# Order of two groups of fetches on GpSimd's queue, and of a latent's sums on TensorE

## The chip, the cores and the metric

The kernel runs on one core of a Trainium2 chip. The metric is the device time of one execution in microseconds (us), and the median over several runs counts.

## The reference

Two transformer blocks run one after the other on a sequence of 1024 positions with 1024 features, all in float32. The change lies in the first block, which reads in short:

```python
x = layer_norm(x, ln_emb_g, ln_emb_b)
z = x @ w_in
xs, gs, cq, ckv, kr, gm = split(z)             # 512, 512, 256, 128, 64, 512 columns
# state-space branch: 32 groups of 16 features with 64 complex states each
y = gelu(scan(xs) + d_skip * xs)
ys = y * sigmoid(y @ w_glu + b_glu) * silu(gs)
# latent attention, 4 heads: 128 plain and 64 rotary columns for queries and keys
q  = rms_norm(cq, q_norm_g) @ w_uq             # rotary(q[..., 128:])
kv = rms_norm(ckv, kv_norm_g) @ w_ukv
k_rope = rotary(kr)                            # one rotary key for all heads
ym = softmax(mask(q @ k.T) * scale) @ v * silu(gm)
u = alpha * x + concat(ys, ym) @ w_out
```

The second block (two more attentions, gates and a gated feed-forward part) follows from it.

## The kernel before, in words

Everything is kept with features on the 128 partitions and positions along the columns. On-chip memory is divided into 50 pages of 1024 float32 columns; a page has several uses one after the other. Each engine runs one instruction list written out by hand, and semaphores tie the lists together. The DMAs that matter here are issued from three lists: SyncE loads weight blocks into a ring of four pages, ACT stores the gates, and GpSimd issues the rest through its software queue.

The stage around the change, in TensorE's order:

- The last two of 16 column tiles of `w_in` (`in_tile(14)`, `in_tile(15)`). ACT takes each from its bank: tile 12 is the key/value latent `CKV`, tiles 13 and 14 are the two pages of the query latent `CQ`, tile 15 is the rotary rows `KR` (and the same rows with their halves exchanged).
- Sums of squares of the latents for their RMS norms. `latent_square_act` (L1003) squares a latent on ACT into `TEMPS_2[i]`, `latent_sums_pe` (L981) sums it with eight small products, `latent_root_act` takes the root, VectorE the reciprocal, and `latent_spread_pe` (L989) spreads it. Latent 0 is the key/value latent, 1 and 2 are the query's. For latents 1 and 2 the squares were both put in page 32, so the second square waits for the first one's sums.
- The state products, four groups `r` (L3282 and L3288), once VectorE says that the states are ready (`states_ready`, L2548). ACT copies each group's result to `UU` (L1929).
- Values and keys from the key/value latent (L3311, and four tiles by the helper at L3125), the four plain query tiles, and the two pairs of rotary query tiles, also at L3125. Of every key and query tile ACT makes a rounded high part, and VectorE the remainder (L2566 for keys, L2584 for queries). The second rotary pair waits for the remainders of all four plain query tiles (`q_low`, 4).
- The gated unit of the state-space branch, four tiles at L3125. It waits for `yg_ready`, the four Gelu activations of ACT (L1952) over `YF` (pages 12 to 15).
- The attention, whose scores begin at L355. It waits for VectorE's `rotary_ready`.

`YF` is the state-space output with features on partitions. `UU` has steps on partitions, so it goes to DRAM and comes back in another layout. GpSimd issues these: the store of `UU` to `y_dram` (L1650), and eight fetches of 256 KB each (L1660) for a quarter of a page's rows at a time. Between store and fetches stand four copies of the rotary rows `KR` (256 KB each, L1654 and L1655) into both halves of pages 46 and 47, and the fetch of the causal mask (L1656). Page 47 holds the half-angle sine until VectorE has made the cosine, so these copies wait for `cm_zero` (L1652), which VectorE reports after the rotary tables are finished (L2571). After the eight fetches have landed GpSimd fetches the gates (L1666, L1667).

VectorE, in its list, waits for the rotary rows (`kr_landed`) after the remainders of the first two plain query tiles. It then makes the rotary key (three operations at L2350, one at L2581, one more at L2350), and only then the last two query remainders:

```python
            for m in range(4):
                if m == 2:
                    dve.wait_ge(S("kr_landed"), 64)
                    dve.wait_ge(S("ssm_ps"), 32)
                    tt(page(46), page(46), COS, ALU.mult)
                    tt(page(47), page(47), SIN, ALU.mult)
                    tt(page(46), page(46), page(47), ALU.add)
                    link(dve.tensor_copy(KRH, page(46)))
                    tt(KRL, page(46), KRH.bitcast(F32), ALU.subtract)
                dve.wait_ge(*T("q_free", m + 1))
                dve.tensor_tensor(QNL[m], two(2 * (m % 2)), QNH[m].bitcast(F32), ALU.subtract).then_inc(S("q_low"), 1)
```

Of the kernel before, what the change touches and what calls it, by code (L numbers as in the profile page):

```python
# [19 lines left out]
PAGE = 1024  # L20
# [7 lines left out]
GROUPS, GC, STATE = 32, 16, 64  # L28
PAIRS = GROUPS // 2
STEP = P // GC  # L30
# [34 lines left out]
def program(nc, t, out):  # L65
    with ExitStack() as ctx:
        sems = {}

        def S(name):
            name = ONE_COUNT.get(name, (name, 0))[0]  # L70
            if name not in sems:
                sems[name] = ctx.enter_context(nc.semaphore(name))
            return sems[name]
# [9 lines left out]
        def cols(a, b, parts=P):  # L83

            if b <= FRONT * PAGE:
                return front[0:parts, a:b]
            return back[0:parts, a - FRONT * PAGE:b - FRONT * PAGE]
# [12 lines left out]
        def page(a, n=1, off=0):  # L100
            return cols(a * PAGE + off, (a + n) * PAGE + off)

        def pages(a, n):
            return page(a, n).rearrange("p (k t) -> p k t", k=n)
# [34 lines left out]
        YF = pages(12, 4)  # L139
# [38 lines left out]
        y_dram = nc.dram_tensor("ssm_out_by_step", (P, GROUPS, CHUNKS), F32, kind="Internal").ap()  # L178
# [203 lines left out]
        def attention_dve(dve, A, bufs, items, per_turn, turns, scale, before):  # L382
            SBUF, PTB = bufs
            n, step, used = len(items), 0, 0
            for what in steps_of(items, per_turn, turns):
# [3 lines left out]
                if isinstance(what, str):  # L389
                    _, dst, times = turns[int(what)]  # L390
                    dve.wait_ge(S(f"{A}_scores"), used)
                    if times is None:
                        dve.tensor_copy(dst, pair).then_inc(S(f"{A}_scores_read"), 1)
                    else:
                        dve.tensor_tensor(dst, pair, times, ALU.mult).then_inc(S(f"{A}_scores_read"), 1)
                    continue
# [354 lines left out]
        def tiles_to(N, k):  # L751
            names = list(NORMS)
            return sum(NORMS[x] for x in names[:names.index(N)]) + k
# [223 lines left out]
        def latent(i):  # L977

            return (CKV, "kv_norm", V("kv_norm_g", 0)) if i == 0 else (CQ[:, i - 1, :], "q_norm", V("q_norm_g", i - 1))

        def latent_sums_pe(pe, i):  # L981
            pe.wait_ge(S("norm_square"), tiles_to("kv_norm", i + 1))
            ones_, at = ones_q if i else ones_kv, 256 if i else 0
            for j in range(4):
                mm = pe.matmul(ps[32 * j:32 * j + 32, 7, at:at + 256], ones_[:, 0:32],
                               TEMPS_2[i][:, 256 * j:256 * j + 256], start=i < 2, stop=i != 1)
            mm.then_inc(S("norm_square_used"), 1)

        def latent_spread_pe(pe, N):  # L989
            pe.wait_ge(S("norm_rstd"), norms_to(N))  # L990
            if N == "q_norm":
                pe.wait_ge(S("norm_scaled"), tiles_to("kv_norm", 1))
            else:
                pe.wait_ge(S("ssm_ps_read"), 24)
            for j in (0, 2, 1, 3):
                at = slice(32 * j, 32 * j + 32)
                if j == 1:
                    mm.then_inc(S("half_spread"), 1)
                    pe.wait_ge(S("half_spread"), 2 if N == "q_norm" else 1)
                mm = pe.matmul(LATENT[:, j, :], pick[at, :], LATENT_ROOT[N][at, :], start=True, stop=True)  # L1000
            mm.then_inc(S("norm_spread"), 1)

        def latent_square_act(act, i):  # L1003
            if i:
                act.wait_ge(S("norm_square_used"), tiles_to("kv_norm", i))
            act.activation(TEMPS_2[i], latent(i)[0], ACT.Square).then_inc(S("norm_square"), 1)

        def latent_root_act(act, N, i):
# [4 lines left out]
        def latent_gain_act(act, i):  # L1013
            x, _, gain = latent(i)
            act.wait_ge(S("norm_scaled"), tiles_to("kv_norm", i + 1))
            act.activation(x, x, ACT.Copy, scale=gain).then_inc(S("norm_ready"), 1)
# [162 lines left out]
                x = quarters(XN[:, k, :])  # L1179
                dve.scalar_tensor_tensor(x, x, V("ln_emb_g", k), SPREAD, ALU.mult, ALU.mult).then_inc(S("norm_scaled"), 1)  # L1180

        TEMPS_2 = (cols(48 * PAGE + 512, 49 * PAGE + 512), page(32), page(32))
        LATENT_ROOT = {"kv_norm": cols(49 * PAGE + 512, 49 * PAGE + 768), "q_norm": cols(33 * PAGE, 33 * PAGE + 256)}
        STATE_BANK = (0, 1, 2, 3)
        K_BANK = (5, 0, 2, 5)
# [115 lines left out]
        def nth(b):  # L1301

            return whole(b) + len(GATES.order) * (b >= B_MERGE + 2 * N_GATES) + len(OUT.order) * (b >= B_UP) + \
                len(UP.order) * (b >= B_DOWN)
# [278 lines left out]
        def _(pool):  # L1583
# [64 lines left out]
            ada_sum(15)  # L1648
            pool.wait_ge(S("ssm_ps_read"), 32)
            pool.dma_start(y_dram, UU).then_inc(S("y_in_dram"), 16)  # L1650
            pool.wait_ge(S("z_free"), N_IN)
            pool.wait_ge(S("dve_step"), DVE_STEP["cm_zero"])  # L1652
            for half in range(2):
                pool.dma_start(page(46)[64 * half:64 * half + 64, :], KR[0:64, :]).then_inc(S("kr_landed"), 16)  # L1654
                pool.dma_start(page(47)[64 * half:64 * half + 64, :], KR[64:128, :]).then_inc(S("kr_landed"), 16)  # L1655
            pool.dma_start(CM[:, SEQ - P:SEQ], t["causal"]).then_inc(S("cm_landed"), 16)  # L1656

            pool.wait_ge(S("y_in_dram"), 16)
            for g in range(8):
                pool.dma_start(YF[g * GC:(g + 1) * GC, :, :].rearrange("c k (s n) -> c k s n", s=STEP),  # L1660
                               y_dram.rearrange("(s c) (k g) n -> g c k s n", c=GC, g=8)[g]).then_inc(S("yf_landed"), 16)
            pool.wait_ge(S("yf_landed"), 16 * 8)
            pool.wait_ge(S("gate_out0"), 64)
            pool.wait_ge(S("gate_out1"), 64)
# [147 lines left out]
        def _(act):  # L1812
# [98 lines left out]
            act.wait_ge(S("dve_step"), DVE_STEP["g_skip"])  # L1911
            act.wait_ge(S("z_free"), 13)
            latent_square_act(act, 0)
            in_high(act, 15)
            z(13, CQ[:, 0, :], ACT.Copy)
            latent_root_act(act, "kv_norm", 0)
            z(14, CQ[:, 1, :], ACT.Copy)
            act.wait_ge(S("z_free"), 15)
            act.wait_ge(S("dve_step"), DVE_STEP["states_ready"])
            latent_square_act(act, 1)  # L1920
            z(15, KR, ACT.Copy)
            latent_square_act(act, 2)
            latent_root_act(act, "q_norm", 2)
            latent_gain_act(act, 0)
# [1184 lines left out]
        def _(pe):  # L3109
# [22 lines left out]
            def ada_column(a, back):  # L3132

                pe.wait_ge(S("ada_summed"), a + 1)
                a0, n = [x for x in ADA_STAGES if x[0] <= a][-1]
                if a == a0 and a > 0:
                    pe.wait_ge(S("ada_read"), ADA_STAGES.index((a0, n)))
                pe.matmul(ps[:, 4, a - a0:a - a0 + 1], ring[:, ADA_BLOCKS[a] % RING, 0:P], ones[:, 0:1],
                          start=True, stop=True).then_inc(S(back), 1)
# [99 lines left out]
            for x in range(16, 24):  # L3239
                pe.wait_ge(S("ssm_ps_read"), x - 9)  # L3240
                q4, i = (x - 16) // 2, x % 2
# [22 lines left out]
            in_tile(14)  # L3264
            in_tile(15)
            pe.sem_inc(S("w_used"), B_UKV)
            latent_sums_pe(pe, 1)
            pe.wait_ge(S("dve_step"), DVE_STEP["states_ready"])
            pe.wait_ge(S("tm_landed"), 16 * (STEP - 1))
            for r in range(4):  # L3270
                if r < 2:
                    pe.wait_ge(S("z_free"), 15 + r)
                else:
                    pe.wait_ge(S("ssm_ps_read"), 22 + 2 * r)

                def state(j, odd):
                    return ps[:, STATE_BANK[2 * (r % 2) + odd], j * P:(j + 1) * P]

                for j in range(4):
                    for odd in range(2):  # L3280
                        g = 8 * r + 2 * j + odd
                        mm = pe.matmul(state(j, odd), TM[:, g, :], UU[:, g, :], start=j == 0, stop=False,  # L3282
                                       skip_group_check=True)
                for j in range(4):
                    for i in range(2):
                        for odd in range(2):
                            h, q = slice(64 * odd, 64 * odd + 64), 4 * r + j
                            mm = pe.matmul(state(j, odd), CP[h, i, q, GC:GC + P], SS[h, i, q, :], start=False,  # L3288
                                           stop=j == 3 and i == 1, skip_group_check=True)
                            if j == 3 and i == 1:  # L3290
                                mm.then_inc(S("ssm_ps"), 1)
                if r == 0:
                    latent_sums_pe(pe, 2)
                    latent_spread_pe(pe, "kv_norm")
                    ada_column(12, "ada_used")
                    ada_column(13, "ada_used")
                elif r == 1:
                    latent_spread_pe(pe, "q_norm")
                    ada_column(14, "ada_used")
                elif r == 2:  # L3300
                    ada_column(15, "ada_used")
# [266 lines left out]
            for i in range(4):  # L3568
                n = nth(B_MERGE + i)
# [13 lines left out]
            for m in range(8):  # L3583
                n, bank = nth(B_MERGE + 2 * N_GATES + m), 4 * (m % 2)
# [80 lines left out]
            for half in range(2):  # L3665
                n = nth(B_UP + 2 + half)
# [158 lines left out]
```

## Time and profile before

| | us |
|---|---|
| median of 3 runs | 2158.92 |
| lowest and highest run | 2156.01, 2160.89 |
| the profiled execution | 2164.66 |
| its span | 2162.8 |
| TensorE busy in the span | 2079.2 |
| VectorE, ACT, GpSimd busy | 1357.9, 818.0, 1141.4 |

The profile is of one execution, and its times count from the span's start. PE is TensorE, DVE is VectorE, POOL is GpSimd, SPq and the like are an engine's instruction queue. An idle time in square brackets stands before the instruction of its row, with what ended it. "x32" is the number of instructions merged in a row.

### The profile page before, as it was taken

The numbers are of one execution on the slowest core, as the hardware profiler recorded it, in microseconds if no ns is written. First come the engines' busy times: TensorE is split into PE (matmuls) and PEld (weight loads), VectorE is DVE, ScalarE is ACT, GpSimd is POOL, SyncE is SP. The second block draws the span as 40 slices with busy tenths as digits, with TensorE's granted clock in tenths as the row PEclk, the third lists the DMA queues.
The fourth block names the chain that finished last, engine by engine and source line by source line (L and its number), as shares of the span: only waits on it lengthen the run. The fifth ranks groups of instructions, "written<-read, shape, count | busy, mean of one in ns | idle before, by whom it ended". The sixth has DMA issues, their size and how long they took to land.

```text
span 2162.8 us, 28447 instructions
## 1 busy us (share of the span) xinstructions
PE 2079.2 (96%) x11124; PEld 1632.0 (75%) x11124; DVE 1357.9 (63%) x1705; ACT 818.0 (38%) x1304; POOL 1141.4 (53%) x793
## 2 busy tenths in 40 slices
PE   8999989999998999999999999998999999999997
PEld 5878745878875885578857788876788888887885
DVE  7999865541768015520067424775977777778988
ACT  6232242340117005620065343134544545453443
POOL 2576713057873663346646764374677778750000
PEclk9999999999998999999999999999999999999999
DMA  7463472042232321001211325333122222137543
GB/s 298 149 142 108 115 158 77 1 185 98 88 102 81 119 78 47 28 27 52 74 24 51 113 100 202 107 117 136 35 74 88 88 88 88 64 135 283 169 152 113
DMA packets 72726, 230.02 MB, mean 106 GB/s; under 512 B 15960, under 2 KB 18824, under 8 KB 71280
## 3 DMA queue, kind: packets, MB, share of 16 engines
q1 hardware_dynamic: 59632, 170.04, 23.8%
q10 hardware_dynamic: 9104, 36.45, 4.6%
q0 software_dynamic: 3856, 21.70, 4.0%
q8 instruction: 89, 1.46, 0.3%
q14 instruction: 45, 0.36, 0.1%
HBM read 180.03 MB, written 46.17 MB: 105 GB/s over the span
## 4 chain that ended last, share of the span: by engine, by line
PE 74%; DVE 16%; ACT 4%; issue 2%; POOL 2%; DMA 2%; SPq 0%; ACTq 0%; DVEq 0%; POOLq 0%
PE ps L3563 22%; PE ps L3160 17%; PE ps L3678 8%; DVE back L2350 6%; PE ps L3487 4%; PE ps L3596 4%; PE ps L3634 2%; PE ps L355 2%; PE ps L3125 2%; PE ps L525 1%; PE ps L513 1%; PE ps L378 1%; PE ps L1050 1%; DMA back<-ssm_out_by_step 1%; PE ps L507 1%
## 5 line engine op out<-in xcount | busy, mean ns | idle before, releaser
L1779 POOL TENSOR_TENSOR up_parts<-front,up_parts 128x512 fp32r<-128x512 f32 x120 | 188.5, 1580 | 74.8 <-ACT up_parts L2087 74.0
L3678 PE MATMUL ps<-ffn_parts,w_parts 128*128 128x512 f32 x924 | 212.6, 392 | 5.0 <-DVE ffn_parts L2946 5.0
L3678 PEld LDWEIGHTS ps<-ffn_parts,w_parts 128*128 128x128 f32 x924 | 174.2, 189 | 42.7 <-DVE w_parts L2938 3.8
L3563 PE MATMUL ps<-t_high,up_parts 128*128 128x512 f32 x640 | 204.0, 390 | 1.2 <-ACT back L2094 0.8
L3160 PE MATMUL ps<-h_high,w_parts 128*128 128x512 f32 x672 | 187.7, 394 | 0.6 <-PE ps L3487 0.6
L1704 POOL TENSOR_TENSOR w_parts<-front,sb_zero 128x1024 fp32r<-128x1024 f32 x48 | 101.9, 2123 | 158.4 <-PE ps L3487 58.1
L3563 PE MATMUL ps<-h_high,up_parts 128*128 128x512 f32 x480 | 154.8, 389 | 0.3 <-DVE back L2755 0.2
L1709 POOL TENSOR_TENSOR w_parts<-front,w_parts 128x1024 fp32r<-128x1024 f32 x54 | 141.9, 2628 | 19.9 <-ACT w_parts L2252 7.5
L3160 PEld LDWEIGHTS ps<-h_high,w_parts 128*128 128x128 f32 x672 | 124.0, 188 | 25.8 <-issue 1.4
L3563 PEld LDWEIGHTS ps<-t_high,up_parts 128*128 128x128 f32 x640 | 120.1, 188 | 27.1 <-issue 1.5
L1590 POOL TENSOR_TENSOR front<-front,sb_csilu 128x1024 f32<-128x1024 f32 x48 | 102.6, 2137 | 61.2 <-DMA front<-w_ada 61.1
L2350 DVE TENSOR_TENSOR back<-back 128x1024 f32<-128x1024 f32 (+10 forms) x72 | 104.9, 1457 | 36.9 <-ACT back L1984 19.5
L1594 POOL TENSOR_TENSOR front<-front 128x512 f32<-128x512 f32 x96 | 120.9, 1259 | 7.5
L3563 PE MATMUL ps<-t_low,up_parts 128*128 128x512 f32 x320 | 124.5, 389 | 0.0
L3563 PEld LDWEIGHTS ps<-h_high,up_parts 128*128 128x128 f32 x480 | 90.1, 188 | 19.7 <-issue 1.1
L3160 PE MATMUL ps<-h_low,w_parts 128*128 128x512 f32 x336 | 103.8, 390 | 0.0
L2755 DVE TENSOR_TENSOR back<-ps,back 128x512 f32<-128x512 f32 x78 | 53.1, 681 | 79.9 <-PE ps L3563 49.4
L2922 DVE SCALAR_TENSOR_TENSOR back<-back,sb_vec 128x1023 f32<-128x1023 f32 x40 | 60.8, 1519 | 52.0 <-ACT back L2232 52.0
L3563 PE MATMUL ps<-h_low,up_parts 128*128 128x512 f32 x240 | 93.4, 389 | 0.0
L2925 DVE SCALAR_TENSOR_TENSOR back<-back,sb_vec 128x1023 f32<-128x1023 f32 x40 | 86.6, 2166 | 1.4
L2094 ACT ACTIVATE back<-ps 128x512 f32<-128x512 f32 x98 | 57.9, 590 | 76.9 <-PE ps L3563 76.8
L614 POOL TENSOR_SCALAR back<-back,sb_na_inv 128x512 f32<-128x512 f32 x64 | 43.8, 698 | 81.6 <-DVE sb_na_inv L580 81.6
(445 smaller groups left out, 5039.6 us busy)
## 6 DMA issues: line engine op xcount, KB each, us to landing
front<-w_ada SPq DMA_DIRECT2D x48, 512.0 KB, 3.6
front<-w_up SPq DMA_DIRECT2D x44, 512.0 KB, 4.2
front<-w_down SPq DMA_DIRECT2D x22, 512.0 KB, 3.7
back<-w_down SPq DMA_DIRECT2D x22, 512.0 KB, 4.4
front<-w_in SPq DMA_DIRECT2D x16, 512.0 KB, 3.9
front<-w_out SPq DMA_DIRECT2D x16, 512.0 KB, 4.5
residual<-back ACTq DMA_DIRECT2D x2, 4096.0 KB, 14.9
front<-w_gates SPq DMA_DIRECT2D x16, 512.0 KB, 4.2
```

The source lines that it names most:

```text
L1590: pool.tensor_tensor(rows, rows, csilu[:].unsqueeze(2).to_broadcast((P, FT, P)), ALU.mult)\
L1594: pool.tensor_tensor(x[:, 0:w], x[:, 0:w], x[:, w:2 * w], ALU.add).then_inc(S("ada_step"), 1)
L1704: pool.tensor_tensor(high, raw, zero[:, 0:1].to_broadcast((P, PAGE)), ALU.add)\
L1709: pool.tensor_tensor(low, raw, high.bitcast(F32), ALU.subtract).then_inc(S("w_split"), 1)
L1779: pool.tensor_tensor(parts[:, BANK:], src, parts[:, 0:BANK].bitcast(F32), ALU.subtract)\
L2350: link(dve.tensor_tensor(o, a, b, op))
L2925: dve.scalar_tensor_tensor(y[:, :SEQ - 1], src[:, 1:], one(conv, n + ((4 + half) * N_UP)), y[:, :SEQ - 1], ALU.mult, ALU.add).then_inc(S(" ...
L3160: mm = pe.matmul(ps[:, bank + nt, :], w_[:, k * P:(k + 1) * P], x_[k][:, nt * BANK:(nt + 1) * BANK], start=k == 0 and n == 0, stop=k == FT ...
L3487: mm = pe.matmul(ps[:, 2 * j + nt, :], WR[n % 2 + w_][:, at:at + P], x_[2 * b + k][:, nt * BANK:(nt + 1) * BANK], start=b == 0 and k == 0 ...
L3563: mm = pe.matmul(o, parts[:, at + k * P:at + (k + 1) * P], x, start=p in (1, 2, 5) and k == 0 and q == 0, stop=k == 3 and q == 2, skip_gro ...
L3596: mm = pe.matmul(ps[:, bank + k // 4 * 2 + nt, :], WR[n % 2 + w_][:, k * P:(k + 1) * P], x_[k][:, nt * BANK:(nt + 1) * BANK], start=k % 4 ...
L3678: mm = pe.matmul(ps[:, (4 if p in (2, 5, 3) else 0) + m, :], weights[:, w_ * BANK + m * P:w_ * BANK + (m + 1) * P], half_of(x, x_), start= ...
```

## The change

Three things change. GpSimd issues the eight fetches of the states, with the wait for the store's landing, directly behind the store, and the rotary rows and the mask behind them. TensorE takes the sums of latent 1 behind the first group of state products and ahead of the sums of latent 2, instead of before that group. The square of latent 2 goes to page 34, and ACT's wait for the former latent's sums falls away.

```diff
         def latent_square_act(act, i):
-            if i:
-                act.wait_ge(S("norm_square_used"), tiles_to("kv_norm", i))
             act.activation(TEMPS_2[i], latent(i)[0], ACT.Square).then_inc(S("norm_square"), 1)
...
-        TEMPS_2 = (cols(48 * PAGE + 512, 49 * PAGE + 512), page(32), page(32))
+        TEMPS_2 = (cols(48 * PAGE + 512, 49 * PAGE + 512), page(32), page(34))
...
             pool.wait_ge(S("ssm_ps_read"), 32)
             pool.dma_start(y_dram, UU).then_inc(S("y_in_dram"), 16)
+            pool.wait_ge(S("y_in_dram"), 16)
+            for g in range(8):
+                pool.dma_start(YF[g * GC:(g + 1) * GC, :, :].rearrange("c k (s n) -> c k s n", s=STEP),
+                               y_dram.rearrange("(s c) (k g) n -> g c k s n", c=GC, g=8)[g]).then_inc(S("yf_landed"), 16)
             pool.wait_ge(S("z_free"), N_IN)
             pool.wait_ge(S("dve_step"), DVE_STEP["cm_zero"])
             for half in range(2):
                 pool.dma_start(page(46)[64 * half:64 * half + 64, :], KR[0:64, :]).then_inc(S("kr_landed"), 16)
                 pool.dma_start(page(47)[64 * half:64 * half + 64, :], KR[64:128, :]).then_inc(S("kr_landed"), 16)
             pool.dma_start(CM[:, SEQ - P:SEQ], t["causal"]).then_inc(S("cm_landed"), 16)
-
-            pool.wait_ge(S("y_in_dram"), 16)
-            for g in range(8):
-                pool.dma_start(YF[g * GC:(g + 1) * GC, :, :].rearrange("c k (s n) -> c k s n", s=STEP),
-                               y_dram.rearrange("(s c) (k g) n -> g c k s n", c=GC, g=8)[g]).then_inc(S("yf_landed"), 16)
             pool.wait_ge(S("yf_landed"), 16 * 8)
...
             pe.sem_inc(S("w_used"), B_UKV)
-            latent_sums_pe(pe, 1)
             pe.wait_ge(S("dve_step"), DVE_STEP["states_ready"])
...
                 if r == 0:
+                    latent_sums_pe(pe, 1)
                     latent_sums_pe(pe, 2)
                     latent_spread_pe(pe, "kv_norm")
                     ada_column(12, "ada_used")
```

## Rows read from the trace of the kernel before

**Rows 1.** The page: span, and the last chain's shares by engine.

```profile
span 2162.8 us, 28447 instructions
PE 74%; DVE 16%; ACT 4%; issue 2%; POOL 2%; DMA 2%; SPq 0%; ACTq 0%; DVEq 0%; POOLq 0%
```

**Rows 2.** The last chain in order of time, 225 to 345: start, us, what.

```profile
251.25 0.03 DVEq L2548
...
251.35 1.07 ACT back L1006
...
252.46 0.64 PE ps L985 x8
...
298.52 19.46 DMA back<-ssm_out_by_step
...
318.01 3.90 ACT back L1952 x4
```

**Rows 3.** Timeline of PE, 235 to 475: start, us, instruction, idle before.

```profile
257.00 0.64 PE L985 MATMUL ps<-back,sb_ones_q 128*32 128x256 f32 x8
...
303.34 13.97 PE L3125 MATMUL ps<-back,front 128*128 128x512 f32 x32 [0.40 <-PE ps L3125]
321.96 16.49 PE L3125 MATMUL ps<-back,front 128*128 128x512 f32 x32 [4.65 <-ACT back L1952]
...
352.87 0.36 PE L355 MATMUL ps<-k_high,q_high 128*128 128x256 f32 x1
```

**Rows 4.** Windows of PE: us, PE busy (count), PEclk, DMA share, GB/s.

```profile
320.00:321.00 1.00, 0.00 (x0) 0.59 0.78 164
...
326.00:327.00 1.00, 1.00 (x2) 0.50 0.96 360
327.00:328.00 1.00, 1.00 (x4) 1.00 1.01 414
...
473.00:474.00 1.00, 0.56 (x2) 0.89 1.15 492
...
477.00:478.00 1.00, 1.00 (x5) 0.90 0.80 344
```

**Rows 5.** Timeline of POOL, 245 to 325.

```profile
274.64 0.61 POOL L1650 DMA_DIRECT2D ssm_out_by_step<-back  x1 [8.77 <-ACT back L1929]
291.52 0.53 POOL L1654 DMA_DIRECT2D back<-back  x1 [16.27 <-DVEq L2572]
...
294.13 5.43 POOL L1660 DMA_DIRECT2D back<-ssm_out_by_step  x8
318.27 0.79 POOL L1666 DMA_DIRECT2D back<-first_gates  x1 [18.71 <-DMA back<-ssm_out_by_step]
```

**Rows 6.** DMA view, 274.6 to 281.3: issues, KB each, us to landing.

```profile
ssm_out_by_step<-back POOLq DMA_DIRECT2D x1, 2048.0 KB, 6.6
```

**Rows 7.** Timeline of ACT, 235 to 345.

```profile
253.22 1.05 ACT L1006 ACTIVATE back<-back 128x1024 f32<-128x1024 f32 x1
```

**Rows 8.** DMA view, 291.5 to 318.1: queue, packets, MB, share of 16 engines; issues.

```profile
q0 software_dynamic: 992, 3.21, 85.0%
q1 hardware_dynamic: 144, 0.52, 9.7%
...
front<-w_out SPq DMA_DIRECT2D x1, 512.0 KB, 15.2
```

**Rows 9.** DMA view, 303 to 313: the only data queue with a row.

```profile
q0 software_dynamic: 357, 1.16, 104.3%
```

**Rows 10.** Timeline of DVE, 297 to 345.

```profile
298.91 3.74 DVE L2350 TENSOR_TENSOR back<-back 128x1024 f32<-128x1024 f32 x3 [0.53 <-DMA back<-back]
...
304.68 2.35 DVE L2584 TENSOR_TENSOR q_low<-ps,q_high 128x1024 fp32r<-128x1024 f32 x2
310.48 2.48 DVE L2350 TENSOR_TENSOR back<-ps,back 128x1024 f32<-128x1024 f32 x2 [3.45 <-PE ps L3125]
```

**Rows 11.** The second and fourth row copy (L1655): issue to landing.

```profile
DMA to landing us min/median/max: 4.1/5.0/5.8
```

## The prediction

> **What bounds the kernel now.** The page's shares of the chain that ended last come first: 74% of it is TensorE's [rows 1]. So a change pays only where TensorE stands still, or stops standing still, on that chain. The chain, read in order of time around the changed lines, has one place that is not an engine at work. The last of the eight transfers that bring the states back from DRAM is out for 19.46 us, and the four Gelu activations follow it [rows 2]. TensorE's timeline shows what this costs: the second pair of query rotary products ends at 303.34 + 13.97 = 317.31 and the gated unit's products start at 321.96, a gap of 4.65 us [rows 3]. The granted clock then adds a second cost. It falls during that gap and is at half speed (1.2 instead of 2.4 GHz) until 327.0, so that 5.04 us of products at half speed do 2.52 us of work [rows 4]. Gap and clock together cost 7.2 us. The attention starts at 352.87 [rows 3], and everything later hangs on it.
>
> GpSimd's timeline says why the states come so late. Their store is issued at 274.64 [rows 5] and lands 6.6 us later, at 281.24 [rows 6]. The first fetch is issued only at 294.13, because the four rotary-row copies (from 291.52 on) and the mask stand ahead of it [rows 5], and these wait for the rotary tables.
>
> **The change, part by part.**
>
> *First latent sums behind state group 0.* VectorE reports the states ready at 251.25, but TensorE waits for the square, which ACT ends at 252.42 and whose sums take 0.64 us; the state products start at 253.10 [rows 2]. Afterwards they can start when ACT could, at 251.35: 1.75 us earlier. The eight sums then stand beside the third latent's. That group's row says 0.64 us [rows 3], and a little of it overlaps with its neighbours, so the net is between 1.1 and 1.2 us; I take 1.2. Nothing eats this up: squares and copies on ACT are done in time (the last square is at 253.22 + 1.05 = 254.27 [rows 7], the sums start at 255.3 at the earliest). So TensorE, ACT's copies, the store to DRAM and the rotary tables all come 1.2 us sooner.
>
> *Second square in a page of its own, its wait gone.* The square that waited starts at 253.22 [rows 7], 0.12 us after the sums on which it waited end (253.10 [rows 2]). The removed wait is worth between 0 and 0.1 us; I take 0. Its purpose is to allow the first edit: otherwise the square would wait for sums that have moved behind the state group.
>
> *Fetches ahead of the rotary rows.* The same 13 transfers are issued, in another order. The store now lands at 281.24 - 1.2 = 280.04. GpSimd resumes 0.28 us after a landing (317.99 to 318.27 [rows 2, 5]), so the first fetch goes out at 280.3 and the last by 285.8 (5.43 us for eight [rows 5]). The wait for the rotary tables ends as before, less 1.2, so the rotary rows are still issued from 291.52 - 1.2 = 290.3. They are issued no later, but behind 2 MB of states in the same queue (eight times 256 KB). No other work on GpSimd is queued behind this wait except the fetch of the gates, which waits for the states in both versions.
>
> How long does the queue take? From the first issue at 291.52 to the last landing at 317.98 are 26.46 us. In that stretch the software queue used 85.0% of 26.6 us of all 16 engines, and the hardware queue 9.7%, that is 2.6 us for 0.52 MB, one weight block [rows 8]. The same work started at 280.3 ends at 306.8. The mask (64 KB) is the last of it; as an estimate I take off 0.5 us for it and have the rotary rows landing at 306.3 if one weight block is served before them, at 303.7 if none is, and at 308.9 if two are. Two are asked for in that time (one of the gated unit, one of the output). For none speaks that the one output block asked for in that stretch took 15.2 us to land [rows 8], and that from 303 to 313 the software queue alone used 104.3% [rows 9], with no row for the hardware queue beside it. For one speaks that the block did move before the queue had drained. I take 305.0, in the middle. The states themselves need at most until 304 and their Gelu 3.9 us more [rows 2], so they no longer set anything.
>
> *What is late next.* VectorE waits for the rotary rows ahead of the last two query remainders, and the second rotary product pair on TensorE waits for those remainders, since it reuses their banks. Before, the rows were there at 298.9, the five rotary operations ran to 304.68 and the remainders to 307.03 [rows 10], ahead of TensorE, which reached the second pair at 303.34 + 6.98 = 310.32 [rows 3]. Now: rows at 305.0, five operations (5.77), two remainders (2.35), small steps between engines (0.1) give 313.2. TensorE gets there at 310.32 - 1.2 = 309.1. So a new gap of 4.1 us opens in place of the old one, one product pair earlier.
>
> *The sum.* Second pair 6.98 us. Clock loss 2.5 us again, as for a gap of like length [rows 4]. Step to the gated unit 0.35. From its start to the attention's it is 352.87 - 321.96 = 30.91 [rows 3], less the 2.52 that the clock took, so 28.4. Together 313.2 + 7.0 + 2.5 + 0.35 + 28.4 = 351.4, against 352.87. The gain is **1.4 us**. VectorE's two rotary passes over the queries have seven operations each, none above the 1.24 us of their first two [rows 10], so the second pass, which can start at 313.2 + 7.0 + 2.5 = 322.7, ends by 331.4, far ahead of 351. The gates, fetched behind the rotary rows, land before TensorE's first gated tile is through, so VectorE's multiplications wait for nothing new. From the attention on the shift is handed down by TensorE.
>
> In one formula: gain = 306.4 minus the landing of the rotary rows, plus 2.5 minus the clock loss. With 303.7 and 308.9 this gives a gain of 2.7 and a loss of 2.5. The clock loss is bounded from below by another gap: after 2.0 us of idleness the clock was at half from about 473.9 to 477.1, 3.2 us, a loss of 1.6 [rows 4]; from above I allow 3.3. Both ends together: 3.6 us faster to 3.3 us slower.
>
> The profiled execution took 2164.66 us with a span of 2162.8 [rows 1]; the sum gives 2163.3 for it. The median of the runs is 5.7 us below that execution, and the difference is carried over: 2158.9 - 1.4 = 2157.5 us. This kernel's runs lie within about 0.1% of their median, so some 0.2% (4.3 us) can be told from no change.
>
> **The rivals.**
>
> *A: the wait moves to the rotary rows (my forecast), 0.50.* 1.4 us faster, own range 3.6 faster to 2.5 slower: 2155.3 to 2161.4.
>
> *B: the rotary rows aren't held up, 0.12.* If they pass the states in the queue and land near 299 as before, TensorE has no gap: second pair 309.1 to 316.1, gated unit from 316.4 at full clock, end 344.8. That is 8.1 us faster, 2150.8. Against it: before, the transfers landed in the order of their issue. The four row copies were through by 298.9 (the fourth 5.8 us after issue), the last states at 318.0, 19.5 after theirs [rows 2, 11]. The Trainium skill (DMA: Bandwidth & Descriptors, section on queues, rings and completion order) says that each engine takes descriptors in ring order but that completion need not follow issue; the first half would hold the rows behind the states, the second would let them overtake by a few packets at most.
>
> *C: the weights are served first, 0.18.* The mechanism is the share of the hardware queue. If both blocks get their turn while the software queue is full, the rotary rows land at 308.9 and the kernel is 2.5 us slower, 3.3 with the longer clock loss: 2161.4 to 2162.2. It decides from a landing after 306.4, and passes 0.2% from 310.7 on. Against it stands the starved output block [rows 8, 9]. The Trainium skill (same page and section) has each engine go round its queues packet by packet; by that rule both blocks would be through before the rotary rows, and the time would be this rival's. The 104.3% to nothing between 303 and 313 speaks against the rule for packets of this shape.
>
> *D: a gap is left, but the clock stays up, 0.20.* A gap shortened to 3 or 4 us in another place may end before the granted clock falls, or find it back sooner. Then up to 2.5 us more are gained: 3.9 faster, 2155.0, at the edge of what can be measured. Against it: the clock fell even for a gap of 2.0 us [rows 4].
>
> That the first edit brings nothing is inside A: every 0.1 us that it fails to give moves the end by as much, 1.2 at most.
>
> **How the numbers follow.** Faster by over 0.2%: all of B, under half of D, a little of A: 0.24. Slower by over 0.2%: part of C (0.07) and the tail of A: 0.10. Within: 0.66. The range reaches from B's 2150.8 to just above C: 2151 to 2162.5.
>
> **What would show it.** State products start near 251.4. First fetch issued near 280.3, rotary rows still near 290.3. VectorE's longest wait in this stretch is for the rotary rows, ended near 305. TensorE's gap before the gated unit is gone and one of about 4 us stands between the two rotary pairs, with the clock at half behind it. The attention starts near 351.5. I am wrong if VectorE's wait ends before 301 (B) or after 309 (C), or if a gap before the attention hands the shift back.

## The result

The change makes the kernel slower. Seven runs have a median of 2170.35 us (2164.00 to 2171.26), and seven of the kernel before 2158.92 us. The ratio is 1.0043, with a 95% interval from 1.003 to 1.0057, so 9.3 us more, where 1.4 us less had been forecast (the two medians alone lie 11.4 us apart). The profiled execution of the changed kernel is the fastest of its seven (2164.00 us, span 2162.2, 6.4 us below their median), and that of the kernel before lies 5.7 us above its median, so the two spans alone hide the loss. The loss shows in the place of the change.

The last chain, in order of time (start, us, what), answers to [rows 2]:

```profile
251.52 2.05 PE ps L3278 x16
...
292.01 17.27 DMA back<-back
309.30 1.24 DVE back L2347
```

The states' fetches have left the chain, and a copy of rotary rows stands in their place, out for 17.27 us. GpSimd's timeline answers to [rows 5]:

```profile
280.45 5.39 POOL L1651 DMA_DIRECT2D back<-ssm_out_by_step  x8 [6.28 <-DMA ssm_out_by_step<-back]
290.46 0.55 POOL L1656 DMA_DIRECT2D back<-back  x1 [4.61 <-DVEq L2569]
...
304.18 0.77 POOL L1663 DMA_DIRECT2D back<-first_gates  x1 [11.06 <-DMA back<-ssm_out_by_step]
```

VectorE's timeline answers to [rows 10]:

```profile
309.30 3.75 DVE L2347 TENSOR_TENSOR back<-back 128x1024 f32<-128x1024 f32 x3 [11.99 <-DMA back<-back]
...
315.07 2.35 DVE L2581 TENSOR_TENSOR q_low<-ps,q_high 128x1024 fp32r<-128x1024 f32 x2
```

TensorE's timeline answers to [rows 3]:

```profile
302.26 7.11 PE L3122 MATMUL ps<-back,front 128*128 128x512 f32 x16 [0.41 <-PE ps L3122]
317.57 7.71 PE L3122 MATMUL ps<-back,front 128*128 128x512 f32 x11 [8.20 <-DVE q_low L2581]
...
356.12 0.35 PE L355 MATMUL ps<-k_high,q_high 128*128 128x256 f32 x1 [0.15 <-PE ps L3122]
```

The rotary rows are issued at 290.46, as forecast, and VectorE gets them at 309.30, after 12 us of waiting. The gap before the gated unit is gone, but one of 8.20 us stands before the second rotary pair. The clock falls in it and comes back 5.5 us after the restart, as windows of TensorE show (us, busy and count, clock, DMA share, GB/s); they answer to [rows 4]:

```profile
312.00:313.00 1.00, 0.00 (x0) 0.93 0.98 393
313.00:314.00 1.00, 0.00 (x0) 0.50 1.05 418
...
323.00:324.00 1.00, 1.00 (x4) 0.95 0.00 0
```

The DMA view of 280.4 to 309.4 answers to [rows 8]. `w_glu` is the gated unit's weight block and `w_out` the output's. The first, asked for at 286.2, needed 18.6 us, and the second 8.9; in the median the rows needed 16.2.

```profile
q0 software_dynamic: 993, 3.22, 82.4%
q1 hardware_dynamic: 256, 0.98, 15.8%
...
back<-back POOLq DMA_DIRECT2D x4, 256.0 KB, 16.2
front<-w_glu SPq DMA_DIRECT2D x1, 512.0 KB, 18.6
front<-w_out SPq DMA_DIRECT2D x1, 512.0 KB, 8.9
```

### The profile page after: what moved, and what is told of

It reads as the page before. It is cut to its first block, busy times and chain, and to the rows that moved or that the text cites. A ratio compares the mean times of both kernels' runs of the same rounds, so it can differ in the third digit from the quotient of the medians.

```text
span 2162.2 us, 28447 instructions
## 1 busy us (share of the span) xinstructions
PE 2076.8 (96%) x11124; PEld 1630.1 (75%) x11124; DVE 1357.9 (63%) x1705; ACT 817.7 (38%) x1304; POOL 1139.3 (53%) x793
## 4 chain that ended last, share of the span: by engine, by line
PE 74%; DVE 16%; ACT 4%; issue 2%; DMA 2%; POOL 2%; SPq 0%; ACTq 0%; DVEq 0%; POOLq 0%
PE ps L3560 22%; PE ps L3157 17%; PE ps L3675 8%; DVE back L2347 6%; PE ps L3484 4%; PE ps L3593 4%; PE ps L3631 2%; PE ps L3122 2%; PE ps L355 2%; PE ps L525 1%; PE ps L513 1%; PE ps L378 1%; PE ps L507 1%; PE ps L650 1%; PE ps L662 1%
## 5 line engine op out<-in xcount | busy, mean ns | idle before, releaser
L1706 POOL TENSOR_TENSOR w_parts<-front,w_parts 128x1024 fp32r<-128x1024 f32 x54 | 142.5, 2639 | 20.8 <-ACT w_parts L2249 7.5
L1599 POOL TENSOR_TENSOR w_in_low<-front,w_in_high 128x1024 fp32r<-128x1024 f32 x16 | 44.1, 2759 | 80.9 <-ACT w_in_high L1107 80.9
```

The source lines that it names most:

```text
L1706: pool.tensor_tensor(low, raw, high.bitcast(F32), ALU.subtract).then_inc(S("w_split"), 1)
```

## The experiments

All compare with runs of the kernel before on the same chip. The table gathers what the traces show: first fetch's issue, last fetch's landing, the time at which VectorE takes the rotary rows, TensorE's idle time before the second rotary pair and before the gated unit, the first score of the attention, the span, and the ratio of the runs. For a landing hidden behind other work GpSimd's next issue less 0.28 us stands.

| kernel | first fetch | states | rows | gaps | attention | span | ratio (interval) |
|---|---|---|---|---|---|---|---|
| before, first profile | 294.13 | 318.0 | 298.9 | 0, 4.65 | 352.87 | 2162.8 | |
| before, second (e5) | 293.97 | 315.4 | 298.8 | 0, 2.19 | 349.47 | 2161.6 | 1.0002 (0.999 to 1.0013) |
| before, third (e6) | 293.51 | 315.4 | 298.4 | 0, 2.70 | 347.83 | 2156.2 | |
| changed, first | 280.45 | 303.9 | 309.3 | 8.20, 0 | 356.12 | 2162.2 | 1.0043 (1.003 to 1.0057) |
| changed, second (e7) | 281.19 | 307.1 | 313.1 | 11.32, 0 | 358.68 | 2166.6 | 1.005 (1.0034 to 1.0067) |
| sums only (e1) | 293.75 | 313.7 | 298.5 | 0, 0.76 | 346.13 | 2154.4 | 0.9994 (0.9981 to 1.0006) |
| fetches only (e2) | 281.14 | 305.1 | 310.5 | 8.76, 0 | 356.19 | 2166.6 | 1.0052 (1.0035 to 1.0068) |
| key last (e3) | 281.20 | 305.3 | 310.7 | 0, 2.16 | 347.51 | 2156.6 | 1.0008 (0.9996 to 1.002) |
| rows between (e4) | 280.51 | 311.0 | 300.8 | 0, 0 | 344.98 | 2152.6 | 0.9988 (0.9977 to 0.9999) |
| rows on SyncE (e8) | 280.33 | 305.2 | 310.9 | 10.02, 0 | 357.25 | 2169.1 | 1.0052 (1.0035 to 1.0068) |
| weights wait (e9) | 282.70 | 305.5 | 310.6 | 7.29, 0 | 356.45 | 2165.1 | 1.0033 (1.0022 to 1.0044) |
| between, weights wait (e10) | 281.95 | 309.3 | 299.9 | 0, 0 | 346.41 | 2155.1 | 0.9985 (0.9976 to 0.9994) |
| before, weights wait (e11) | 295.18 | 316.0 | 300.3 | 0, 1.64 | 348.44 | 2156.7 | 0.9994 (0.9984 to 1.0003) |
| older source (e12) | 280.41 | 305.6 | 312.3 | 11.21, 0 | 358.80 | 2168.0 | 1.005 (1.0032 to 1.0069) |

**Each half of the change alone.** The first kernel keeps the sums and the page and puts the fetches back; the second moves only the fetches.

```diff
 e1_sums_only, against the changed kernel
             pool.dma_start(y_dram, UU).then_inc(S("y_in_dram"), 16)
-            pool.wait_ge(S("y_in_dram"), 16)
-            for g in range(8):
-                pool.dma_start(YF[...], y_dram...)
...
             pool.dma_start(CM[:, SEQ - P:SEQ], t["causal"]).then_inc(S("cm_landed"), 16)
+            pool.wait_ge(S("y_in_dram"), 16)
+            for g in range(8):
+                pool.dma_start(YF[...], y_dram...)
```

> The change without the moved fetches: rows, mask and then the fetches, as before; the sums of latent 1 behind state group 0 and the second square in page 34 are kept. Theory 1 (the held-up rotary rows are the whole cause of the loss): everything up to the attention comes 1.0 to 1.2 us sooner, the rows land near 297.7, the attention starts near 351.7 against 352.87, and the time is 1 us shorter than before, which can't be told from no change. Theory 2 (the sums or the new page cost something later, for instance a bank or page that another engine needs): the head start is gone by the attention, and the time is 3 us or more longer than before.

> The fetches moved ahead of the rotary rows, the sums and the squares as before. Theory 1 (held-up rows): the rows land near 309.3 + 1.1 = 310.4, a gap of about 8 us stands before the second rotary pair, the attention starts near 357, 4 us later than before, and the time is slower than before by as much as the whole change or 1 us more, 4 to 11 us. Theory 2 (sums or page are to blame): the time is that of before, within 4 us.

The loss is all with the fetches: 1.0052 for them alone, 0.9994 for the sums alone, whose interval holds both their 1.2 us and nothing. The attention of the fetches alone starts at 356.19, behind a gap of 8.76 us, near the 357 and 8 of theory 1. VectorE and TensorE of the fetches alone:

```profile
310.53 3.75 DVE L2350 TENSOR_TENSOR back<-back 128x1024 f32<-128x1024 f32 x3 [12.55 <-DMA back<-back]
```

```profile
318.80 8.69 PE L3125 MATMUL ps<-back,front 128*128 128x512 f32 x16 [8.76 <-DVE q_low L2584]
```

The profile of the sums alone brought a surprise. Its attention starts 6.7 us sooner than in the first profile of before, where 1.2 was expected. Most of that isn't the sums: with the same queue order the fetches landed 20.0 us after their first issue instead of 23.9, and TensorE hardly waited. ACT and TensorE of it:

```profile
313.76 3.90 ACT L1949 ACTIVATE back<-back 128x1024 f32<-128x1024 f32 x4 [8.83 <-DMA back<-ssm_out_by_step]
```

```profile
317.71 14.00 PE L3122 MATMUL ps<-back,front 128*128 128x512 f32 x32 [0.76 <-ACT back L1949]
```

**Is the first profile typical?** Three more profiles of unchanged kernels.

> The kernel before, unchanged, profiled once more. In the first profile the eight fetches took 24 us from first issue to last landing and in the one with the sums alone 20 us, with the same order on the queue; the attention started at 352.87 and at 346.13. Theory 1 (the first profile of the kernel before is not typical in this place): the fetches take about 20 us here, the gap before the gated unit is under 2 us, the clock stays up in it, and the attention starts near 347 to 348. Rival (moving the sums is worth more than its 1.2 us): the fetches take 24 us again and the attention starts near 352.

> The kernel before, unchanged, a third profile, to see how far the landing of the fetches and the granted clock behind them vary between executions. Theory 1: fetches about 20 us, attention near 347 to 348. Rival: fetches 24 us, attention near 352.

> The changed kernel, unchanged, profiled once more. Theory 1 (the rotary rows, held up behind the states, set the start of the attention): the rows land 27 to 30 us after the first fetch is issued, near 309, whatever the clock does, the gap before the second rotary pair is 8 us, and the attention starts at 355.5 to 357.5. Rival (the loss varies as the fetches do in the kernel before): in one of two profiles the rows land near 305 and the attention starts before 353.

TensorE in the second and in the third profile of before:

```profile
319.35 15.70 PE L3125 MATMUL ps<-back,front 128*128 128x512 f32 x32 [2.19 <-ACT back L1952]
```

```profile
319.40 14.00 PE L3125 MATMUL ps<-back,front 128*128 128x512 f32 x32 [2.70 <-ACT back L1952]
```

Both gaps are about half of the 4.65 us of [rows 3]. In the third profile the first two gated tiles take 14.00 us, so the clock stayed up, while the second profile lost 1.7 us to it. The attention starts at 349.47 and 347.83, between the two theories' figures and nearer to the first; the three profiles give 350.1 on average. The changed kernel's second profile has a longer gap than its first:

```profile
313.14 3.75 DVE L2347 TENSOR_TENSOR back<-back 128x1024 f32<-128x1024 f32 x3 [15.11 <-DMA back<-back]
```

```profile
321.40 8.57 PE L3122 MATMUL ps<-back,front 128*128 128x512 f32 x16 [11.32 <-DVE q_low L2581]
```

Its attention starts at 358.68, later than the 357.5 that was given as the bound, so the landing varies here too, but upward. The changed kernel's two profiles average 357.4. That is 7.3 us behind the kernel before, most of the 9 to 11 us that the runs show. The second of them is within 1 us of the median of its runs (2168.43 against 2167.93), where the first was 6.4 us below it; with the second alone the distance is 8.6 us. What follows the attention's start takes 1806 to 1812 us in every trace of the table, with no order among the kernels, so the rest can't be placed with so few traces.

**Take the rows off TensorE's path.** VectorE makes the last two remainders first and the rotary key behind them.

```diff
             for m in range(4):
-                if m == 2:
-                    dve.wait_ge(S("kr_landed"), 64)
-                    tt(page(46), page(46), COS, ALU.mult)
...
                 dve.wait_ge(*T("q_free", m + 1))
                 dve.tensor_tensor(QNL[m], two(2 * (m % 2)), QNH[m].bitcast(F32), ALU.subtract).then_inc(S("q_low"), 1)
+            dve.wait_ge(S("kr_landed"), 64)
+            tt(page(46), page(46), COS, ALU.mult)
...
```

> The changed kernel, but VectorE makes the last two query remainders ahead of its wait for the rotary rows, and the rotary key behind them. The rows land as late as in the changed kernel, but nothing on TensorE waits for them. Theory 1: no gap before the second rotary pair, which starts near 309.3; the gated unit follows at 316.4 at full clock and the attention starts near 345, 8 us sooner than before and 11 us sooner than in the changed kernel; the time is 5 to 11 us shorter than before. Rival (late rows hurt in another place, the query rotations or the attention's first scores): the attention starts near 350 or later, and the time is within 3 us of before.

VectorE and TensorE:

```profile
310.71 3.75 DVE L2347 TENSOR_TENSOR back<-back 128x1024 f32<-128x1024 f32 x3 [5.80 <-DMA back<-back]
```

```profile
302.99 13.97 PE L3121 MATMUL ps<-back,front 128*128 128x512 f32 x32 [0.40 <-PE ps L3121]
319.12 13.97 PE L3121 MATMUL ps<-back,front 128*128 128x512 f32 x32 [2.16 <-DVEq L2585]
```

The rows are as late as in the changed kernel, and the gap before the second pair is gone (32 products in a row); the attention starts 8.6 us sooner than in the changed kernel's first profile. This shows that the late rows acted through the two remainders. The rival had a point as well. The rotary key now stands ahead of the first query rotation, which must empty the banks for the gated unit, and TensorE waits 2.16 us for that (`qr_free`). So the time is that of before (1.0008, interval 0.9996 to 1.002), and the 5 to 11 us expected did not come.

**Fetch half, rows, fetch half.**

```diff
-            for g in range(8):
+            for g in range(4):
                 pool.dma_start(YF[...], y_dram...)
...
             pool.dma_start(CM[:, SEQ - P:SEQ], t["causal"]).then_inc(S("cm_landed"), 16)
+            for g in range(4, 8):
+                pool.dma_start(YF[...], y_dram...)
```

> The changed kernel with four of the eight fetches ahead of the rotary rows and the mask, and four behind them. Theory 1 (the queue is served in the order of issue): four fetches of some 2.3 us each from 281.8 are through near 291.5, so the rows issued at 290.3 land near 298, as before; the last fetch lands near 306, its Gelu ends near 310, ahead of TensorE at 316. No gap of over 2 us, the attention near 345, the time 5 to 11 us shorter than before. Rival (it is the amount of work asked of the queue in the stretch, not its order): the rows land after 303 still, and the time is within 4 us of before.

VectorE and TensorE:

```profile
300.80 3.74 DVE L2350 TENSOR_TENSOR back<-back 128x1024 f32<-128x1024 f32 x3 [3.45 <-DMA back<-back]
```

```profile
302.31 13.97 PE L3125 MATMUL ps<-back,front 128*128 128x512 f32 x32 [0.40 <-PE ps L3125]
316.58 13.97 PE L3125 MATMUL ps<-back,front 128*128 128x512 f32 x32 [0.30 <-PE ps L3125]
...
344.98 0.35 PE L355 MATMUL ps<-k_high,q_high 128*128 128x256 f32 x1 [0.15 <-PE ps L3125]
```

The same 13 transfers with the rows in the middle: no gap at all, and the attention at 344.98 as expected. The landings were later than expected (the rows at 300.8 and not 298, the last fetch at 311.0 and not 306), and TensorE was just covered. Of the rows on GpSimd's queue, then, what stands ahead of them decides, and the rival of the mere amount of work falls. The gain in time, 0.12% or 2.6 us of 2158 (interval from nearly nothing to 5), is below the 5 to 11 us expected. A part of the difference is that the kernel before is typically better than its first profile; but against the 350.1 of its three profiles the attention starts 5.1 us sooner here, so a rest stays unexplained.

**The rows on another queue.**

```diff
             load(B_GLU + 1, None, *tile_of(t["w_glu"], 1))
+            sp.wait_ge(S("z_free"), N_IN)
+            sp.wait_ge(S("dve_step"), DVE_STEP["cm_zero"])
+            for half in range(2):
+                sp.dma_start(page(46)[...], KR[0:64, :])...
+                sp.dma_start(page(47)[...], KR[64:128, :])...
...
             pool.wait_ge(S("dve_step"), DVE_STEP["cm_zero"])
-            for half in range(2):
-                pool.dma_start(page(46)[...], KR[0:64, :])...
-                pool.dma_start(page(47)[...], KR[64:128, :])...
```

> The changed kernel, but SyncE issues the four rotary-row copies, behind the second weight block of the gated unit, so that they are on the hardware queue and not behind the fetches in the software queue. Theory 1 with the trace's sign that the hardware queue is served little while the fetches run: the rows land after the weight block, near 303 to 308, hardly sooner than in the changed kernel, and the gap is 3 to 8 us. Rival (only the order within the software queue holds the rows up): they land near 298, there is no gap, the attention starts near 345 and the time is 1 to 3 us shorter than before.

SyncE's issues and VectorE:

```profile
289.77 0.54 SPq L1438 DMA_DIRECT2D back<-back  x1
...
291.63 0.60 SPq L1439 DMA_DIRECT2D back<-back  x1
```

```profile
310.93 3.75 DVE L2349 TENSOR_TENSOR back<-back 128x1024 f32<-128x1024 f32 x3 [13.80 <-DMA back<-back]
```

Issued by 291.63, the rows are there at 310.93, no sooner than from the software queue, and the gap before the second rotary pair is 10.02 us. The rival falls, and theory 1 had the gap (3 to 8 us) too small and the landing (by 308) too early. While the fetches run (their last lands at 305.2), neither queue gets the rows through. On SyncE's queue, though, the rows stand behind the weight block, which landed at 286.0 + 20.1 = 306.1. Whether they would get through at the head of that queue wasn't tried.

**Were the weight blocks to blame?** SyncE asks for the two blocks only when the fetches (in the first kernel the rows too) have landed.

```diff
             sp.wait_ge(S("w_used"), B_UKV + 1)
+            sp.wait_ge(S("yf_landed"), 16 * 8)
+            sp.wait_ge(S("kr_landed"), 64)      # only in e9
             load(B_GLU + 1, None, *tile_of(t["w_glu"], 1))
```

> The changed kernel, but SyncE asks for the second weight block of the gated unit, and so for the output's first, only once the fetches and the rotary rows have landed. Nothing but the software queue's own work runs from 281 to the rows' landing. Theory 1a (the two weight blocks got ahead of the rotary rows and pushed them back by some 5 us): the fetches land 21 us or less after their first issue and the rows near 304, the attention starts near 350 to 352, and the time is 3 to 7 us shorter than the changed kernel's, 2 to 5 us longer than before. Rival (the fetches are slower when they follow the store at once, whatever else runs): the fetches still take 23 to 25 us and the rows land at 308 or later.

> Four fetches, the rows and the mask, four fetches, and SyncE asks for the two weight blocks only once the fetches have landed. Theory 1a: the last fetch lands 2 to 5 us sooner than the 311.0 of the run with the fetches split alone, so that slower executions have cover too; no gap, the attention near 345 in all of them, the median 2 to 5 us below before. Rival (the gated unit's second block is now late, or the time is limited elsewhere): the median is that of the split alone or worse, within 2 us of before.

> The kernel before, but SyncE asks for the two weight blocks only once the fetches have landed. In the order of before one block moved during the fetches. Theory 1a: the last fetch lands 1 to 3 us sooner than in the three profiles of before (21.4 to 24.0 us after the first fetch's issue), at 19 to 20 us; the time is 0 to 3 us shorter than before. Rival (the fetch's duration varies by itself): 21 to 24 us again.

VectorE and TensorE of the first:

```profile
310.57 3.74 DVE L2349 TENSOR_TENSOR back<-back 128x1024 f32<-128x1024 f32 x3 [11.08 <-DMA back<-back]
```

```profile
318.84 8.91 PE L3124 MATMUL ps<-back,front 128*128 128x512 f32 x16 [7.29 <-DVE q_low L2583]
```

The first fetch goes out at 282.70 here, so the rows land 27.9 us behind it, against 28.8 to 31.9 us in the five profiles with the blocks in the stretch and the rows last on GpSimd's queue (changed twice, e2, e3, e12). By this one trace the blocks cost some 1 to 4 us; the spread of the five is 3 us, so the size isn't settled. Theory 1a had the rows near 304. They came at 310.6, as the rival had it (308 or later). The blocks are a part at most and not the cause, and 1.0033 is still a clear loss. In the order of before the fetches take 20.9 us without the blocks and 20.0 to 23.9 with one in the stretch, so the blocks' part can't be seen there, and the time doesn't change measurably. With the rows between and the blocks waiting, the last fetch lands 27.3 us after the first issue instead of 30.5, there is no gap, and the ratio is 0.9985 (0.9976 to 0.9994). That version beats the kernel before by 3.2 us, with an interval of 1.3 to 5.2. It can't be told from the split alone (0.9988).

**Does it matter what is read?** The eight fetches read another DRAM tensor with the same address pattern, so this kernel leaves the states out of the computation.

```diff
-  y_dram.rearrange("(s c) (k g) n -> g c k s n", c=GC, g=8)[g]
+  x_dram.rearrange("(p a) (b n) -> p (a b) n", a=4, b=8).rearrange("(s c) (k g) n -> g c k s n", c=GC, g=8)[g]
```

> The changed kernel, but the eight fetches read, with the same pattern of addresses, another DRAM tensor of the same size, the state-space input that was written some 180 us earlier, instead of the states stored just before. The output is therefore not the reference's from the first block on. What is open: with the fetches right behind the store each of them takes 2.5 to 2.9 us from landing to landing, in the order of before 1.9 to 2.3 us. Theory A (what has just been written is read more slowly): the step falls to about 2.0 us, the fetches take 19 us or less, the rows land near 304 to 305 and the attention starts 4 to 5 us sooner than in the changed kernel. Theory B (the place in time or the order on the queue sets the rate, not what is read): the step stays at 2.5 us or more and the time is the changed kernel's, 8 to 11 us longer than before.

Its fetches, from issue to landing, against those of the changed kernel's first profile:

```profile
DMA to landing us min/median/max: 5.8/12.8/20.8
```

```profile
DMA to landing us min/median/max: 5.3/11.7/19.0
```

The step from landing to landing is (4.7 + 20.8 - 5.8) / 7 = 2.8 us, 4.7 us being the time between the first and the last issue. It stays that of the changed kernel (2.6 and 2.9 us in its two profiles), and so does the time, 1.005. So what is read isn't the reason.

## Why the prediction was wrong

**The mechanism was right.** The state products start at 251.52 (251.4 forecast), the first fetch goes out at 280.45 (280.3), the rows at 290.46 (290.3). The states land at 303.9 (at most 304), the gap moves from the gated unit to the second rotary pair, and the rotary rows are what VectorE waits for. The wait ends at 309.30, just past the 309 that the prediction gave as its sign of being wrong. Rival B falls with that landing. The clock fell in all six profiles with a gap before the second pair (changed twice, e2, e8, e9, e12): the pair takes 8.6 to 9.9 us there, and 7.0 at full clock. So rival D didn't come true; but its gap of 3 to 4 us never arose there, the six are of 7.3 to 11.3 us.

**The step that failed first: "The same work started at 280.3 ends at 306.8".** This term put the rows' landing at 305.0 with an upper end of 308.9. The 13 transfers, which took 26.5 us in the first profile of before, take longer in the new order, though they took only 22.6 to 24.5 us in the four later profiles of the old one (e5, e6, e1, e11). Measured from the first issue to the rows they took 28.8 and 31.9 us, that is to 309.3 and 313.1. Of this the weight blocks may explain 1 to 4 us (e9). Without them 27.9 us are left, where the old order without them needs 316.04 - 292.58 = 23.5 us for everything (e11). The fetches by themselves are slower in the new place: step 2.6 and 2.9 us, against 1.9 to 2.4 in the order of before. With the rows at 309.3 the formula of the prediction gives a loss of 2.9 us, plus 0.4 for the clock, 3.3 in all. The trace shows 356.12 - 352.87 = 3.25. So the formula held and its input was wrong by 4 to 8 us.

**The step that failed second: the state of before was read from one execution.** The prediction took the gap of 4.65 us and the clock's 2.5 us from it as what there was to win. Two further profiles have gaps of 2.19 and 2.70 us, and clock losses of 1.7 and 0. Their attention starts at 349.47 and 347.83, so in a typical execution of before 3 to 5 us less were to be won. The sentence "The profiled execution took 2164.66 us ... the median of the runs is 5.7 us below that execution, and the difference is carried over" passed over a sign: an execution 5.7 us above the median had lost those microseconds somewhere, and about 3 of them before the attention. The sign is a weak one, though: the second profile was 5.1 us above the median of its runs (2163.37 against 2158.25), with a gap of only 2.19 us. Both errors point the same way. Against the typical before of 350.1 the new order costs 6 to 9 us at the attention's start.

**Rival C** had the right side with a fitting landing (308.9), and part of the right reason: the first weight block was through at 304.8, before the rows, the second at 310.9, behind them. Its price of 2.5 us was too low for the same second error, and e9 shows that its mechanism carries a part only.

**The sums** gave what was forecast where VectorE's report of the states came last. From its last step before the report to the second group of state products there are 8.3 us in the five profiles with the old sums and 7.0 in six with the new ones (first profiles: 251.14 to 259.43, and 251.34 to 258.36). In the three others (e4, e7, e9) there are 7.9, and TensorE goes on there without a pause: it reached the products later than the report, a case that the prediction didn't have. Alone the gain can't be told from noise in the runs.

**Still open:** why the fetches are slower in the new order. Each of them writes 16 of the 128 partitions in all four pages of `YF`. From 286 to 296 the software queue moved 98 to 107 GB/s (0.98 to 1.07 MB) in all seven profiles with the eight fetches right behind the store. In the five of the order of before it was 116 to 146 GB/s (0.93 to 1.17 MB from 303 to 311, or 304 to 312 in e11). It isn't what they read (e12: 99), nor the weight blocks (e9: 105, and a step of (4.7 + 18.3 - 5.6) / 7 = 2.5 us). In the changed kernel the weight queue moved nothing in that stretch anyway: the DMA view of 286 to 296 has one queue with a row.

```profile
q0 software_dynamic: 327, 1.07, 104.3%
```

It isn't simply the place behind the rows either: the last four fetches of the two split kernels stand there too and moved at 107 GB/s (e4 from 301 to 307, e10 from 300 to 306). A fetch that waits for some microseconds behind the store, with nothing ahead of it, wasn't tried.

## What to carry to other kernels

When a fetch is moved up in a queue, look for the next consumer of whatever it overtakes, and follow that consumer's own queue: here a copy of 1 MB, wanted near 297, went behind 2 MB that nobody could use before 312, and held two small remainders and through them TensorE. Splitting the large group around the small one gave both their time, where either whole order left a gap. And before a gap is counted as what can be won, get a second and a third trace: the same gap was 4.65, 2.19 and 2.70 us in three executions of one kernel. A profiled execution that lies off its median by as much as the gap is a reason to do so, but not a measure of the gap.

## What the runs showed of the hardware

- The duration of the same eight fetches in the old order on the queue varied from 20.0 to 23.9 us between executions (e1 and the first profile of before), more than most effects under study.
- Transfers on the hardware queue (SyncE's) got through very slowly beside the fetches: the 512 KB weight block took 18.6 us in the changed kernel and 3.4 in the first profile of before, where nothing else ran beside it; the rows issued by SyncE took 18 to 19 us.
- The weight block had to wait before its first packet. In the changed kernel it was asked for at 286.2, with all eight fetches issued, and its queue moved no packet before 297; then its 144 packets went through by 304.8, beside 240 of the software queue. In e4, with four fetches issued, it was asked for at 286.25, and its first packets went between 290 and 291. The Trainium skill (DMA: Bandwidth & Descriptors, section on queues, rings and completion order) has the engines go round their queues packet by packet. From 297 on the trace fits that rule, with more than one packet in three for the block. The eleven microseconds before don't fit it, unless the block's packets weren't ready, which the trace doesn't show. The changed kernel's DMA view of 297 to 304.8:

```profile
q0 software_dynamic: 240, 0.79, 60.5%
q1 hardware_dynamic: 144, 0.52, 39.9%
```

- The granted clock after like gaps differed: after 2.16 us (e3) and 2.70 us (e6) of idleness it stayed at 2.4 GHz, after 2.19 us it was at 1.2 GHz for a while (e5). Windows of TensorE in the second and the third profile of before:

```profile
321.00:322.00 1.00, 1.00 (x2) 0.50 1.02 414
```

```profile
321.00:322.00 1.00, 1.00 (x3) 1.00 1.08 438
```
